# Odd layer's attention: key tiles turned in other PSUM banks, a third page buffer, copies and low parts dealt out anew

## What is computed

```python
qn, kvc, kvs, kvw, gates, qd, kvd, qi, ki, wi = split(x @ w_in, O_SIZES)
kc, vc = blocks_of_64(kvc) weighted by w_cmp          # compressed branch "c"
o_c = softmax(qn kc - slope * dist) vc
o_s = softmax(qn ks - slope * dist) vs                # selected branch "s"
o_w = softmax(qn kw - slope * dist, window) vw        # window branch "w"
o_n = gate_c * o_c + gate_s * o_s + gate_w * o_w
isc = sum_h relu(qi ki) * wi                          # indexer
o_d = softmax(qd kd - slope * dist over top_k(isc)) vd  # branch "d"
out = concat(o_n, o_d) @ w_out
```

## Time and profile before

| | us |
|---|---|
| median of 3 runs | 1495.02 |
| lowest and highest | 1493.78, 1502.56 |
| the profiled execution | 1494.26 |
| its span, first to last instruction | 1492.7 |
| mean granted TensorE clock | 0.972 |
| PE busy | 1412.9 |
| DVE busy | 794.5 |
| ACT busy | 497.8 |
| POOL busy | 393.2 |

### The profile page before, as it was taken

One profiled execution on the slowest core, in us unless ns is written; L12 is line 12 of the kernel. 1 busy time (PEld: TensorE's weight loads), 2 busy tenths in 40 slices (PEclk: granted clock), 3 DMA queues, 4 the chain that ended last, 5 costly groups with the idle time before them and its releaser, 6 DMA issues. The chain is left out here.

```text
span 1492.7 us, 26872 instructions
## 1 busy us (share of the span) xinstructions
PE 1412.9 (95%) x10941; PEld 1331.0 (89%) x10941; DVE 794.5 (53%) x1384; ACT 497.8 (33%) x990; POOL 393.2 (26%) x466
## 2 busy tenths in 40 slices
PE   6999998889999999998899799998989999999996
PEld 5999965889999999997899667887989999999996
DVE  3424877485334343436689757666476343343435
ACT  3322223345222131224432355555354123141221
POOL 3014413473010010127635452001563010010102
PEclk9999999999999999998899899998999999999998
DMA  4423150031331322304233231102132231321301
GB/s 149 141 86 114 49 209 4 3 113 60 111 112 59 114 77 94 113 8 100 85 57 96 58 134 58 57 1 57 58 113 82 89 113 58 113 105 67 114 29 58
DMA packets 87194, 123.82 MB, mean 83 GB/s; under 512 B 24438, under 2 KB 42302, under 8 KB 87040
## 3 DMA queue, kind: packets, MB, share of 16 engines
q1 hardware_dynamic: 82048, 107.00, 22.2%
q0 software_dynamic: 5024, 15.10, 3.3%
HBM read 115.62 MB, written 8.57 MB: 83 GB/s over the span
## 5 line engine op out<-in xcount | busy, mean ns | idle before, releaser
L1014 PE MATMUL ps<-xh,ring_lo 128*128 128x260 f32 (+2 forms) x2496 | 505.2, 285 | 1.4 <-ACT big L1563 1.4
L1014 PEld LDWEIGHTS ps<-xh,ring_lo 128*128 128x128 f32 (+2 forms) x2496 | 385.8, 189 | 3.3 <-ACT big L1563 2.2
L1014 PE MATMUL ps<-xl,wr 128*128 128x260 f32 (+1 forms) x1568 | 353.5, 286 | 16.0 <-POOL xl L807 8.6
L1014 PE MATMUL ps<-xh,wr 128*128 128x260 f32 (+1 forms) x1568 | 355.3, 287 | 10.0 <-POOL xl L801 5.2
L1014 PEld LDWEIGHTS ps<-xl,wr 128*128 128x128 f32 (+1 forms) x1568 | 258.5, 190 | 18.2 <-POOL xl L807 9.4
L1014 PEld LDWEIGHTS ps<-xh,wr 128*128 128x128 f32 (+1 forms) x1568 | 259.3, 191 | 13.0 <-POOL xl L801 5.4
L1920 DVE TENSOR_TENSOR ring_lo<-ring,wr 128x1024 fp32r<-128x1024 f32 (+1 forms) x148 | 196.7, 1332 | 78.8 <-ACT wr L1563 78.6
L819 POOL TENSOR_TENSOR att<-att 128x520 f32<-128x520 f32 (+1 forms) x80 | 76.4, 956 | 556.4 <-DVE att L1944 514.9
L1014 PE MATMUL ps<-hh,wr 128*128 128x260 f32 x1024 | 222.1, 283 | 0.0
L1014 PE MATMUL ps<-hh,ring_lo 128*128 128x260 f32 x1024 | 221.8, 283 | 0.0
L1014 PE MATMUL ps<-hl,wr 128*128 128x260 f32 x1024 | 221.7, 283 | 0.0
(11 more groups left out here) (351 smaller groups left out, 1741.8 us busy)
## 6 DMA issues: line engine op xcount, KB each, us to landing
ring<-in_w_up SPq DMA_DIRECT2D x16, 2048.0 KB, 8.2
ring<-in_w_down SPq DMA_DIRECT2D x16, 2048.0 KB, 7.9
ring<-in_w_in_e SPq DMA_DIRECT2D x9, 1024.0 KB, 5.5
ring<-in_w_in_e SPq DMA_DIRECT2D x2, 2048.0 KB, 8.7
ring<-in_w_out_e SPq DMA_DIRECT2D x2, 2048.0 KB, 8.8
ring<-in_w_in_o SPq DMA_DIRECT2D x16, 256.0 KB, 4.9
ring<-in_w_out_o SPq DMA_DIRECT2D x8, 512.0 KB, 7.3
cbuf<-in_cache_kv POOLq DMA_DIRECT2D x32, 128.0 KB, 2.3
```

Of the source, the lines that this page charges most:

```text
L1014: last = pe.matmul(bank(g, half)[0:width(g), 0:H2], w[:, k, :], x[:, k, cols(half)], start=first, stop=final)
```

## The change

- The eight key tiles are turned in banks 4 to 7, right behind the last projection tile. ACT copies six of them (0, 1, 2, 3, 4, 6), DVE two (5, 7). The scores of units 0 and 1 are issued before the wait for these copies, and the samples' part is turned in banks 2 and 3 after them.
- `top_keys` does two of its steps already at tile 4. `place_compressed` moves from unit step 0 to tile 11, without its last product (`sD`), which goes to step 5. The compressed branch's softmax moves two steps later on all engines, and `sample_queries` from steps 2, 3 and 7 to 9, 10 and 11. `sD` and `VF` get memory of their own.
- A third page buffer x (the ring slot of the kc to vs weights, whose next load now waits for `pvs_mm` 1). Pages to compress go into y first and are multiplied there, then gather 0 goes into x, and gather 2 into c without a wait.
- `compress_cached` is cut into 5, 5 and 6 products at steps 21, 22 and 23 (8 and 8 before), `cached_values` into four parts of 8 products over four steps (two of 16 before). The bases of `STEP` become 10, 19 and 28.
- The output weights' `w_hi` go from steps 80 to 83 to steps 70, 73, 76 and 79, their low parts from DVE to POOL, `y_hi` from steps 84 to 87 to 91 to 94, and four entries of `FINAL_AT` move.

```diff
-FINAL_AT = [27, 29, 43, 45, 73, 75, 83, 85]
+FINAL_AT = [27, 29, 43, 45, 77, 79, 83, 90]
...
         wide_split(512, ("kc", "vc", "ks", "vs"), "w_lo_p")
+        c = len(chunks) - 1
+        chunks[c] = (chunks[c][0], ("pvs_mm", 1))
+        KEYS_SLOT = slot_of(c)
...
-        out_chunks(G_OUT1, out_rows)
+        out_chunks(G_OUT1, out_rows, "w_lo_p")
...
-        STEP = {"s": (10, 4, "y", "n", 0), "d": (18, 8, "c", "d", 2), "w": (26, 12, "y", "n", 3)}
+        STEP = {"s": (10, 4, "x", "n", 0), "d": (19, 8, "c", "d", 2), "w": (28, 12, "y", "n", 3)}
...
-        EARLY = len(units) - 16
+        EARLY, APART, TOKENS_D = len(units) - 26, 3, len(units) - 5
...
 # gpsimd
-            gather(0, kv_page(2 * P), cache["y"])
+            gather(1, kv_page(0), cache["y"])
             pool.wait_ge(sm["mm_b"], G_IN1 + Z["qn3"] + 1)
             gather(4, ...)
-            pool.wait_ge(sm["mm_b"], G_OUT1)
-            gather(1, kv_page(0), cache["c"])
             pool.wait_ge(gat[1], 16 * NT)
             for t in range(NT):
-                last = pool.tensor_tensor(cache["c"][:, t, :], cache["c"][:, t, :], wcK, ALU.mult)
+                last = pool.tensor_tensor(cache["y"][:, t, :], cache["y"][:, t, :], wcK, ALU.mult)
             last.then_inc(sm["cw_ok"], 1)
+            gather(0, kv_page(2 * P), cache["x"])
...
+            gather(2, kv_page(4 * P), cache["c"])
             pool.wait_ge(sm["cmp_mm"], 1)
-            gather(2, kv_page(4 * P), cache["c"])
-            pool.wait_ge(sm["pvs_mm"], 1)
             pool.dma_start(cache["y"], cache_win[0]...).then_inc(gat[3], 16)
             pool.wait_ge(sm["store_c"], 16 * 3 * MH + 16)
             pool.wait_ge(sm["outs"], 16 * 12)
+            for u in range(NS1, NS1 + NW):
+                low_part(u)
...
 # tensor
-            pe.wait_ge(sm["free_a"], G_OUT1)
-            pe.wait_ge(sm["free_b"], G_OUT1)
+            pe.wait_ge(sm["free_a"], G_IN1 + Z["vw"] + 1)
+            pe.wait_ge(sm["free_b"], G_IN1 + Z["vw"] + 1)
             for s, name in enumerate(SLOTS):
                 if s >= 4:
-                    pe.wait_ge(sm["tm_a"] if s % 2 == 0 else sm["tm_b"], (s - 4) // 2 + 1)
+                    pe.wait_ge(sm["tm_a"], s - 3)
                 for i in range(QT):
-                    last = tr(ps[s % 4][:, P * i:P * i + P], big[:, L[name], P * i:P * i + P], P)
+                    last = tr(ps[4 + s % 4][:, P * i:P * i + P], big[:, L[name], P * i:P * i + P], P)
...
             unit_scores(0)
+            unit_scores(1)
+            for s, name in enumerate(SLOTS):
+                last = tr(ps[2 + s // 4][0:B, ...], big[:, L[name], S:T], P)
+            last.then_inc(sm["tms_mm"], 1)
+            pe.wait_ge(sm["tm_a"], 6)
+            pe.wait_ge(sm["tm_b"], 2)
...
 # scalar
-            for s in range(0, 8, 2):
+            for s in (0, 1, 2, 3, 4, 6):
...
-                if EARLY <= t < EARLY + NW:
-                    w_hi(NS1 + t - EARLY, ("pvs_mm", 2))
-                if 0 <= t - EARLY - 4 < NP:
-                    y_hi(NP + t - EARLY - 4, "pb_ev", 7)
+                if t in range(EARLY, EARLY + APART * NW, APART):
+                    w_hi(NS1 + (t - EARLY) // APART, ("pvs_mm", 2))
+                if 0 <= t - TOKENS_D < NP:
+                    y_hi(NP + t - TOKENS_D, "pb_ev", 7)
...
 # vector
+                if idx == 4:
+                    top_keys(2)
                 if 5 <= idx < len(O_NAMES) - 1:
                     top_keys(4)
...
+                if idx == Z["vc"] + 2:
+                    place_compressed()
-            for s in range(1, 8, 2):
+            for s in (5, 7):
...
-                if t == 0:
-                    place_compressed()
-                if t == 4:
+                if t == 5:
+                    link(dve.tensor_tensor(sD.rearrange(c4, i=QT, c=NH), dcv, slop, ALU.mult))
+                if t == 6:
...
-                if EARLY <= t < EARLY + NW:
-                    w_lo(NS1 + t - EARLY)
```

More of the change, by code:

```diff
@@ L253, in build, with out_chunks @@
         NE = len(split)
-        def out_chunks(base, parts_of):
+        def out_chunks(base, parts_of, first="w_lo"):
             for j in range(2):
-                split_chunk(lambda slot: parts_of(slot, 512 * j), range(base + 4 * j, base + 4 * j + 4))
+                split_chunk(lambda slot: parts_of(slot, 512 * j), range(base + 4 * j, base + 4 * j + 4), by="w_lo" if j else first)
         out_chunks(G_OUT0, lambda slot, c0: [(cols_of(slot, 0, KD, 512), rows(w_out_e[0], c0, c0 + 512))])
@@ L550, in build @@
         assert o + 1024 <= SLOT, o
-        pbt = flat[:, len(O_NAMES) * T + QT * 1024 + 1024 + 1152:][:, 0:384]
+        BEHIND = len(O_NAMES) * T + QT * 1024 + 1024 + 1152 + 384
+        pbt = flat[:, BEHIND - 384:BEHIND]
+        assert BEHIND + 512 <= KF * T
         QB = {"d": piece(512), "n": piece(512)}
@@ L1409, in sample_step, with compress_cached, cached_values @@
                         cached_values(cb, 0)
-            def compress_cached(half):
-                for t in range(half * NT // 2, (half + 1) * NT // 2):
-                    last = mm(ps[4][0:32, 0:256], BS[:, 30 - 2 * t:62 - 2 * t], cache["c"][:, t, :],
+                    if k == base + 9:
+                        cached_values(cb, 2)
+            def compress_cached(t0, t1):
+                for t in range(t0, t1):
+                    last = mm(ps[4][0:32, 0:256], BS[:, 30 - 2 * t:62 - 2 * t], cache["y"][:, t, :],
                               start=(t == 0), stop=(t == NT - 1))
                 return last
-            def cached_values(cb, half):
-                for b in range(half * B // 2, (half + 1) * B // 2):
+            def cached_values(cb, quarter):
+                for b in range(quarter * B // 4, (quarter + 1) * B // 4):
                     for t in range(2):
@@ L1426, in sample_rest @@
             def sample_rest(k):
+                if k == 4:
+                    pe.wait_ge(sm["cw_ok"], 1)
+                    pe.wait_ge(sm["bt_ev"], 4)
+                    compress_cached(0, 5)
                 if k == 5:
-                    compress_cached(1).then_inc(sm["cmp_mm"], 1)
+                    compress_cached(10, NT).then_inc(sm["cmp_mm"], 1)
                 for base, n0, where, q, n in STEP.values():
                     if k == base + 8:
-                        cached_values(cache[where], 1).then_inc(sm["pvs_mm"], 1)
+                        cached_values(cache[where], 1)
+                    if k == base + 9:
+                        cached_values(cache[where], 3).then_inc(sm["pvs_mm"], 1)
             def compressed_step(t):
@@ L1459, in unit_scores @@
                 if u == 0:
+                    pe.wait_ge(sm["kz_ok"], 2)
+                if u == first_of[4]:
                     pe.wait_ge(sm["kz_ok"], 6)
-                qn = "qd0" if br == "d" else "qn0"
                 mm(ps[u % 2][:, 0:P * (i + 1 - k0)], big[:, L[f"q{'d' if br == 'd' else 'n'}{p}"], P * i:P * i + P],
@@ L1525, in final_step @@
                     final_added(FINAL_SPLIT)
+            pe.wait_ge(sm["free_a"], G_OUT1)
+            pe.wait_ge(sm["free_b"], G_OUT1)
             unit_scores(0)
+            unit_scores(1)
+            for s, name in enumerate(SLOTS):
+                last = tr(ps[2 + s // 4][0:B, P * (s % 4):P * (s % 4) + P], big[:, L[name], S:T], P)
+            last.then_inc(sm["tms_mm"], 1)
+            pe.wait_ge(sm["tm_a"], 6)
+            pe.wait_ge(sm["tm_b"], 2)
             for t in range(len(units) + 3):
+                if t == 2:
+                    pe.wait_ge(sm["tms_ev"], 2)
                 if 0 <= t - 2 < len(units):
                     unit_turned(t - 2)
-                if t + 1 < len(units):
+                if 1 < t + 1 < len(units):
                     unit_scores(t + 1)
@@ L2411, in sample_queries @@
                     last.then_inc(sm["qb_ok"], 1)
-                if t == 3:
+                if t == 10:
                     place_queries("n")
-                if t == 7:
+                if t == 11:
                     dve.tensor_copy(vals[:, 32:40], big[:, L["vs"], S:T])
```

42 lines of the change are left out of this document (17 added, 25 removed).

## The result

The changed kernel takes a median of **1489.56 us** (1484.20 to 1493.44, 16 runs). The kernel before, run beside it, takes 1499.20 us (1493.78 to 1502.70, 16 runs). The ratio is 0.9932, with a 95% interval from 0.9917 to 0.9947: about 10 us, or 0.7%, faster. The forecast was 14.5 us and 1480.5 us. The measured median lies 0.6 us above the top of the range, 1489.

What follows compares the result with a forecast made beforehand. PE bounds the kernel, busy 95% of the span, with slack only at the entry and the last third. Gains of 6.5 + 8.0 = 14.5 us from 1494.3, plus 0.76 for the median, gave 1480.5 us, range 1474 to 1489.

Steps and rivals of the forecast that it cites:

- The entry up to unit 8: Start of the units: unit 0 scored 8.5 us sooner and turned 9.7 sooner; 6.5 us kept at unit 12.
- The price of POOL beside DVE: Steps 6 to 11: POOL's 16 multiplications beside DVE's work cost 3.5 us, bounds 0 and 11.0.
- The far bound of 11.0 us: Entry: upper bound of POOL's price, all 16 multiplications standing in DVE's way.
- the entry gives little: Rival, chance 0.17: DVE and POOL collide longer or PE's clock falls; entry gains 2 us, time 1485.
- POOL in DVE's way: Rival, chance 0.03: linked DVE commands wait for whole POOL instructions, 20.6 us of moved work; time 1498, slower.
- The buffers and the gathers: Third page buffer, gathers and output weight loads: no PE waits, effect taken as 0, bounds 0 to 2 us.
- The last third: Steps 82 to 87: full clock and no wait would save 10.7 us; less 2.7 of stalls, 8.0 us.
- the two causes: Last third: lots of 16 8-column products before the first clock fall, DVE's closing and low parts before the second.
- The sum: Whole kernel: 6.5 us from the entry plus 8.0 from the last third, 14.5 us, giving 1480.5 us.
- The side of the 1% line: Measurement threshold at 1480.1 us: faster by over 1% 0.44, within 1% 0.53, slower 0.03.
- half of 0.50 and 0.08: Chances of the forecast case, 1477 to 1483 us (0.50), and of more than forecast, 1474.6 us (0.08).

Runs made afterwards that it cites:

- late: The change with gather 0 issued ahead of POOL's 16 multiplications, so they start later; 1489.80 us, ratio 0.9929 to the kernel before.
- link: The change with a semaphore wait between each of POOL's 16 multiplications and the next; 1484.69 us, ratio 0.9887 to the kernel before.
- quarters: The kernel before with only the 8-column value products cut into four parts; 1502.53 us, ratio 1.0036 to the kernel before.
- lots16: The change with the 8-column value products in two lots of 16 again; 1499.59 us, ratio 0.9993 to the kernel before.
- late_link: The change with gather 0 ahead of the multiplications and a semaphore wait between each of them; 1480.47 us, ratio 0.9877 to the kernel before.
- link_c: The change with a semaphore wait between POOL's multiplications, the kernel of link measured a second time; 1480.18 us, ratio 0.9879 to the kernel before.
- late_link_c: The kernel of late_link measured again beside link_c; 1480.80 us, ratio 0.9876 to the kernel before.
- entry_back: The kernel of link with the entry of the kernel before; 1493.16 us, ratio 0.9955 to the kernel before.
- wlo_back: The kernel of link with low parts back on DVE and ACT's high parts back, at steps 80 to 83; 1496.54 us, ratio 0.9971 to the kernel before.
- after_ctl: The changed kernel measured again, unaltered, as control; 1487.99 us, ratio 0.9913 to the kernel before.

## Why the prediction came out as it did

**The entry up to unit 8: right.** Counted from the last projection, unit 0 was scored 8.6 us sooner (forecast 8.5), and turned 9.7 us sooner (845.06 - 826.50 against 837.15 - 828.26; forecast 9.7). DVE's last top-k product came at 832.92 where 831.5 was forecast, but everything stood 1.8 us later before the change began. `place_queries` stayed stuck beside POOL, 3.03 us, as the prediction had assumed. The clock was 1.00 from 829 to 850 us.

**The price of POOL beside DVE: the step that failed.** The prediction took 3.5 us for "some six linked commands and 14 short copies" that meet the 16 multiplications, each losing part of an instruction of 0.69 us. What happened is one instruction that lost 8.6 us (9.06 - 0.43), and a lower clock behind it. From unit 8 to unit 12 the gain fell from 9.8 to -1.9 us. Relative to the last projection unit 12 was thus 0.1 us later than before, where 6.5 sooner was forecast. In late, where no row of POOL stands beside these units, unit 12 comes 8.8 us sooner than in the change, both counted from the last projection. So the term priced at 3.5 us measured 8.8, and 2.0 with the row opened (link). The far bound of 11.0 us was the nearer one.

Two places in the trace of the kernel before bore on this. The first is `place_queries` at 788.88, which took 3.25 instead of 0.80 us. The prediction says that its copies end only when POOL's low part is over, but the low part ends at 790.64 and the copies at 792.13. What lies between are two short POOL copies:

```profile
790.59 1.28 POOL L912 COPY att<-big 64x512 f32<-64x512 f32 x2
```

One DVE copy stood until the low part ended (1.79 us), and one beside each of the two POOL copies (0.64 and 0.52). Each of these three POOL instructions has a semaphore wait in front of it, and DVE got its turn every time. From that the step to "held until each one ends" was fair for such instructions. For a row of 16 without a wait it does not hold, as the rows of this study show: DVE does not get its turn between two of them.

The second is the row of 16 itself, 866.35 to 877.37 in the kernel before. There it did no harm, since until 876.7 DVE had only biases, maxima and a reciprocal beside it, the kinds that run at their usual length. The first instruction of another kind stood until the row ended, 0.68 us instead of 0.17:

```profile
876.72 0.68 DVE L2581 TENSOR_SCALAR small<-small 128x8 f32<-128x8 f32 x1
```

The change moved the row from there to a place beside products with two SBUF inputs.

The rival "the entry gives little" named this collision (gain 2, chance 0.17), with 1485 as its time. The rival "POOL in DVE's way" named the mechanism, but multiplied it by all of POOL's work, the low parts included. The low parts, at 984.70 to 1009.25 one by one and 2.36 us each, cost nothing visible: PE has no wait between 980 and 1012.

The Trainium skill, SBUF — State Buffer, section Who interferes with whom, is more exact than the sentence of the GPSIMD Engine Reference that the prediction weighed. It says that the shared pair of ports is an exclusive lock; that a VectorE instruction with two SBUF inputs contends with a GpSimd instruction that reads SBUF, and one in a two-port mode with GpSimd, where whoever issues first has the pair for the whole instruction; and that a VectorE instruction with at most one SBUF input outside these modes does not contend. The traces agree on who is hit: beside the same row DVE's maximum, one SBUF input, took its usual 0.69 us (849.16) and the two-input product 9.06. On how long they go further than the page's "whole instruction": it was the whole row that remained, some 13 instructions.

**The buffers and the gathers: right about the waits.** No PE wait in the changed profile ends at a gathered page or an output weight's transfer; POOL's second gather was issued before 898. No run takes the third buffer out alone. Its price is not nothing, though: it is the new order of the gathers, pages to compress first, that brings the multiplications from 866.35 to 847.59, and so into DVE's way.

**The last third: right in size, for reasons that don't add up.** From the start of step 80 to the tail it went from 42.2 to 34.0 us, a gain of 8.3 where 8.0 was forecast. The rows of PE in the changed kernel:

```profile
1017.84 1.01 PE L987 MATMUL ps<-ring 128*128 128x8 f32 x8
...
1029.48 0.88 PE L987 MATMUL ps<-big,att 128*128 128x64 f32 x6 [0.82 <-ACT att L1580]
```

Four parts of eight at full clock, and no wait above 0.82 us. The prediction weighed the two causes as if they added up; in the runs the thin lots alone make the last third longer (quarters, 47.8 us), and the moved low parts alone give a part (lots16, 37.3). That the total came out near 8.0 has luck in it. (The working has a slip of 0.1: 6 x 1.3 + 2 x 0.95 is 9.7, not 9.8.)

**The sum.** Forecast 6.5 + 8.0 = 14.5. In the profile: -0.1 at unit 12, -3.1 in the middle (the lower clock at 912), +8.3 in the last third, hence 5.0 in the units' stretch (219.7 to 214.7). The tail gave 2.3 back. The medians differ by more than these two executions, 9.6 us. Part of that is the profile of the kernel before. Its mean clock is 0.972, as in all its executions near 1494 us, while those above 1500 us have 0.964 to 0.967. Between 826 and 862 us the clock was 0.86 in that profile and 0.57 in quarters, with the same entry; the difference over 36 us takes 0.007 from the mean of the whole, and so leads from 0.972 to 0.965. So the old entry most likely costs more in the typical execution than in the one that the prediction read, and the change took that away too. It is an inference: no slower execution of the kernel before was profiled. With the row opened, the units' stretch is 9.6 (link) to 13.3 us (late_link) shorter than before, next to the forecast 14.5, and in medians link is 14.1 us faster than the kernel before beside it, late_link and link_c 21.0 and 21.9. So once the row is opened, the gain is not short of the forecast any more.

**The median shown.** The prediction was anchored at a median of 1495.02 from three runs; sixteen runs gave 1499.20. This shift of 4.2 us works against the kernel's time, not against the ratio: 0.9932 of 1495.02 would have been 1484.9, inside the range. The forecast's own ratio was 0.9903. The side of the 1% line is the one that the prediction held likelier; its chances for the two sides don't follow from its cases, though, since half of 0.50 and 0.08 are 0.33 for over 1% faster, where it has 0.44.

## What to carry to other kernels

Before moving GpSimd work beside VectorE work, look at how it is issued as well as at how much it is: a row of instructions without a semaphore wait between them can hold one small VectorE instruction to the row's end, and a wait between each, 2 us in all here, opens it. Price a collision by the length of the whole row, not of one instruction, and look which VectorE instructions the row will stand beside: the same row cost nothing in its old place. Where a stretch suffers from a low TensorE clock, edits to it need not add up (the thin lots here lost 5 us without the other edit and gained 2 to 3 with it), so test them together and one by one. And before a profile is used as the base, see where its time lies among the runs of its kernel.

## What the runs showed of the hardware

- A row of 16 GpSimd multiplications (10.96 us) held a VectorE `tensor_tensor` with two SBUF inputs for 9.06 us (0.43 elsewhere) and a `tensor_scalar` of 8 columns for 7.60 us (0.17 elsewhere). VectorE instructions with one input in PSUM, `tensor_reduce` and `reciprocal` ran at their usual length beside it (0.67, 0.69, 0.20 us). With a semaphore wait between the multiplications the same two took 0.44 and 0.74 us (link, late_link_c).
- TensorE fully busy ran at 1.2 GHz for 14 us (entry_back, 842 to 856) after a stretch with waits, and for 6 us (wlo_back, 1018 to 1024). In lots16 the clock fell to 1.2 GHz with PE busy for 9.00 of 9.00 us (a mean of 0.62 from 945 to 954), in the second of two lots of 16 products with 8 columns. The kernel before has such lots at a clock of 1.00 as well. A full timeline of PE is no proof of a full clock.
- Two executions of one kernel differ by a whole stretch at the lower clock: link and link_c by the one at 903 us, the change and after_ctl by the one at 912. The old entry has it at 0.97 (the kernel before) or 0.50 (entry_back, quarters) from 842 to 856. So a profile against a profile tells no difference under 3 us or so; stretches measured between two fixed events do better than absolute times.
